# First stage of a float32 layer pair: tile by tile, with x's root applied in the turn, and the values' weights first

## What is computed

```
n = rmsnorm(h, g_mix)          # x * rsqrt(mean(x*x) + EPS) * g
proj = n @ w_in                # 1024 columns in, 6704 out
(b_gate, c_gate, h_conv, q, k_c, v_c, k_s, v_s, k_w, v_w, g_br, g_conv, g_attn) = split(proj)
```

## Time and profile before

| | us |
|---|---|
| median of 3 runs | 745.41 |
| lowest, highest | 744.83, 745.76 |
| the profiled execution's own time | 745.85 |
| its span | 744.1 |
| PE busy in the span | 739.4 (99%) |
| DVE busy, ACT busy | 517.9 (70%), 415.9 (56%) |

### The profile page before, as it was taken

The page is one execution under the profiler, slowest core; times in us unless marked ns, Lnnn a source line. Parts: engine busy times, 40 slices in busy tenths (PEclk is TensorE's granted clock), DMA queues, the critical chain, the costliest instruction groups (busy, mean ns, idle before and its releaser), DMA issues.

```text
span 744.1 us, 11570 instructions
## 1 busy us (share of the span) xinstructions
PE 739.4 (99%) x4557; PEld 640.3 (86%) x4557; DVE 517.9 (70%) x834; ACT 415.9 (56%) x788; POOL 66.5 (9%) x103
## 2 busy tenths in 40 slices
PE   9999999999999999999999999999999999999998
PEld 8999989877788888888888888887888888888886
DVE  5784777795756677887367757898667777447762
ACT  6475557456454456565356547697646656346640
POOL 7300000000010000530000004400100000000000
PEclk9999999999999999999999999999999999999999
DMA  8998454343355546656655562735355655656511
GB/s 261 296 316 270 94 116 147 113 151 114 133 170 197 182 150 219 201 211 227 190 174 203 170 226 60 253 117 179 109 166 170 195 200 175 221 169 193 203 57 56
DMA packets 99209, 131.26 MB, mean 176 GB/s; under 512 B 5357, under 2 KB 79163, under 8 KB 99156
## 3 DMA queue, kind: packets, MB, share of 16 engines
q1 hardware_dynamic: 96564, 125.58, 52.5%
q0 software_dynamic: 2304, 4.43, 2.7%
q10 hardware_dynamic: 288, 0.52, 0.2%
HBM read 128.68 MB, written 1.84 MB: 175 GB/s over the span
## 4 chain that ended last, share of the span: by engine, by line
PE 97%; DVE 2%; ACT 1%; issue 0%; POOL 0%; POOLq 0%
PE B L1631 39%; PE B L1597 22%; PE B L1602 11%; PE B L1586 11%; PE B L1812 2%; PE B L1859 2%; PE B L1822 2%; PE B L1644 1%; PE B L1695 1%; DVE LO L1007 1%; PE B L1638 1%; PE B L1815 1%; PE B L1839 1%; PE B L1740 1%; PE B L1798 0%; PE B L1739 0%
## 5 line engine op out<-in xcount | busy, mean ns | idle before, releaser
L1007 DVE TENSOR_TENSOR LO<-RAW,HI 128x1024 fp32r<-128x1024 f32 x236 | 282.4, 1235 | 100.7 <-ACT HI L543 100.2
L1631 PE MATMUL B<-HI,AA 128*128 128x512 f32 (+1 forms) x960 | 286.4, 376 | 0.3 <-DVE AA L1013 0.2
L543 ACT ACTIVATE HI<-RAW 128x1024 fp32r<-128x1024 f32 (+1 forms) x240 | 236.9, 1038 | 61.4 <-PE B L1631 57.8
L1631 PEld LDWEIGHTS B<-HI,AA 128*128 128x128 f32 x960 | 175.7, 188 | 33.0 <-issue 1.1
L1597 PE MATMUL B<-AA,HI 128*128 128x512 f32 x704 | 179.2, 393 | 0.0
L1631 PE MATMUL B<-LO,AA 128*128 128x512 f32 (+1 forms) x480 | 178.5, 372 | 0.0
L1597 PEld LDWEIGHTS B<-AA,HI 128*128 128x128 f32 x704 | 126.7, 189 | 23.0 <-issue 0.7
L1631 PEld LDWEIGHTS B<-LO,AA 128*128 128x128 f32 x480 | 90.6, 189 | 14.7
L1602 PEld LDWEIGHTS B<-AA,LO 128*128 128x128 f32 x704 | 96.6, 190 | 7.1
L1602 PE MATMUL B<-AA,LO 128*128 128x256 f32 x704 | 98.8, 282 | 0.0
L1586 PE MATMUL B<-AA,HI 128*128 128x256 f32 x448 | 83.1, 286 | 0.0
(11 more groups left out here) (313 smaller groups left out, 634.1 us busy)
## 6 DMA issues: line engine op xcount, KB each, us to landing
RAW<-in_w_in SPq DMA_DIRECT2D x29, 1024.0 KB, 5.5
RAW<-in_w_gate SPq DMA_DIRECT2D x22, 1024.0 KB, 5.4
RAW<-in_w_up SPq DMA_DIRECT2D x22, 1024.0 KB, 5.4
RAW<-in_w_down SPq DMA_DIRECT2D x22, 1024.0 KB, 5.0
RAW<-in_w_in SPq DMA_DIRECT2D x10, 512.0 KB, 6.3
RAW<-in_w_attn_out SPq DMA_DIRECT2D x4, 1024.0 KB, 5.1
RAW<-in_w_o SPq DMA_DIRECT2D x4, 1024.0 KB, 5.0
RAW<-in_w_out SPq DMA_DIRECT2D x4, 1024.0 KB, 5.0
```

Of the source, the lines that this page charges most:

```text
L543: e.activation(pieces(HI, NSPL, i, k), pieces(RAW, NRAW, i, k), ACT.Copy).then_inc(split_hi, 1)
L1007: e.tensor_tensor(pieces(LO, NSPL, i, k), pieces(RAW, NRAW, i, k), pieces(HI, NSPL, i, k), ALU.subtract).then_inc(split_lo, 1)
L1631: x = e.matmul(dst, a, w[:, t, c0:c0 + n], start=(first and t == 0 and k == 0), stop=(last and t == nk - 1 and k == 2))
```

## The change

- x's quarters and unit 0 are transferred in another order and by other queues: SP takes x(0,1), the gain row, x(1,0), x(1,1) and the second half of unit 0; ACT's queue takes x(0,0) and then the first half of unit 0.
- Unit 0 is now the values' weights; the keys' is unit 1, and all up to the values' old place move by one.
- Means and roots are made for each tile apart. The root's factor is no longer multiplied into `TOK`; DVE multiplies it into the identity (`root_turner`: PT is 128x128), and PE's turn is a float32 matmul of TOK with that diagonal (`first_turn`), not a transpose. The turns go by tile: (0,0), (0,1), (1,0), (1,1).
- PE makes the values first, in quarters of 4 products by tile, half of x and kind (AH x hi, AH x lo, AL x hi), twelve quarters of 4; the bias rows stand between two of them. The keys follow as 6 groups of 8. `idle` has 9, 1 and 3 where it had 14, 3, 7 and 3.
- On POOL both roots now stand ahead of the transfers into VR.
- The values at the end of the queries are gone; the first piece of `fill()` is made there instead, ahead of the waits for the queries' copies, and step 0 of the loop makes one piece where it made two.

```diff
@@ SP
-            for h in range(2):
-                e.dma_start(X[:, 0, halves(h)], A["x"][0, 0:128, halves(h)]).then_inc(x_in[h], 16)
-                if h == 0:
-                    e.dma_start(GAIN[0:128:64, :], ...
+            e.dma_start(X[:, 0, halves(1)], A["x"][0, 0:128, halves(1)]).then_inc(x_in[1], 16)
+            e.dma_start(GAIN[0:128:64, :], ...
...
-                    e.dma_start(dst[:, 0:4, :], src[:, 0:4, :]).then_inc(unit0_in, 16)
+                    for h in range(2):
+                        e.dma_start(X[:, 1, halves(h)], A["x"][0, 128:256, halves(h)]).then_inc(x_in[2 + h], 16)
@@ ACT
-            for t, h in ((0, 0), (1, 0), (0, 1)):
-                e.wait_ge(x_in[2 * t + h], 16)
-                squares(2 * t, X[:, t, :], QK[:, t, :], h)
+            e.wait_ge(x_in[0], 16)
+            squares(0, X[:, 0, :], QK[:, 0, :], 0, squares0_sb)
             hi(0, 0)
...
+            turned(0, B[5], 0, 0)
+            e.wait_ge(x_in[2], 16)
+            squares(2, X[:, 1, :], QK[:, 1, :], 0, squares_sb, 3)
+            e.wait_ge(x_in[3], 16)
+            squares(2, X[:, 1, :], QK[:, 1, :], 1)
+            turned(1, B[6], 4, 0)
             hi(0, 1)
@@ DVE
+            mean(0).then_inc(mean_sb, 1)
+            e.wait_ge(gain_pe, 1)
             gained(0, 0)
+            root_turner(0)
+            gained(0, 1)
+            lo(0, 0)
+            turned(0, B[5], 0, 0)
+            gained(1, 0)
             e.wait_ge(squares_sb, 4)
+            mean(1).then_inc(mean_sb, 1)
             gained(1, 1)
+            root_turner(1)
+            turned(1, B[6], 4, 0)
             lo(0, 1)
@@ PE
+            first_turn(0)
+            first_turn(1)
+            idle(3)
+            quarter(0, 0, AH, hi, True)
+            quarter(0, 0, AH, lo)
+            quarter(0, 0, AL, hi)
+            e.matmul(B[4][0:4, 0:ROW], REL[:, :], OH[:, :], start=True, stop=True).then_inc(rel_pe, 1)
+            quarter(0, 1, AH, hi)
+            first_turn(2)
+            first_turn(3)
+            quarter(0, 1, AL, hi)
+            quarter(1, 0, AH, hi, True)
+            quarter(1, 0, AH, lo)
+            quarter(1, 1, AH, hi)
+            quarter(0, 1, AH, lo, last=True).then_inc(vals_pe, 1)
+            quarter(1, 1, AH, lo)
...
-            for t in range(2):
-                values(U_VALS, 0, t)
...
+            filler = fill()
+            next(filler)
             e.wait_ge(q_sb, 8)
...
-                for _ in range(FILL_AT[i]):
+                for _ in range(FILL_AT[i] - (i == 0)):
```

More of the change, by code:

```diff
@@ L530, in _ @@
             own = Own(e, act_step)
-            for h in range(2):
-                e.dma_start(X[:, 1, halves(h)], A["x"][0, 128:256, halves(h)]).then_inc(x_in[2 + h], 16)
+            e.dma_start(X[:, 0, halves(0)], A["x"][0, 0:128, halves(0)]).then_inc(x_in[0], 16)
+            src, nk, n = units[0][0:3]
+            dst = RAW[0][:, 0:nk * n].rearrange("p (t n) -> p t n", t=nk)
+            e.dma_start(dst[:, 0:4, :], src[:, 0:4, :]).then_inc(unit0_in, 16)
             def hi(i, k=None):
@@ L1046, in _ @@
-            e.tensor_scalar(TOK[:, 0, halves(0)], TOK[:, 0, halves(0)], ST[:, 6:7], None, ALU.mult).then_inc(scaled_sb, 2)
-            gained(1, 1)
[L1048 to L1052, removed]
+                e.tensor_tensor(TOK[:, t, halves(h)], X[:, t, halves(h)], B[2 + h][:, :], ALU.mult).then_inc(scaled_sb, 1)
@@ L1652, in _, with first_turn @@
             x.then_inc(gain_pe, 1)
[L1653 to L1665, removed]
+            idle(1)
+            def first_turn(n):
+                t, h = n // 2, n % 2
+                e.wait_ge(scaled_sb, n + 1)
+                e.wait_ge(root_diag, t + 1)
+                take(5 + h, turn_lo, n + 1)
+                for j in range(4):
+                    x = e.matmul(B[5 + h][:, 128 * j:128 * j + 128], TOK[:, t, 512 * h + 128 * j:512 * h + 128 * j + 128],
+                                 PT[:, t, 0:128], start=True, stop=True)
+                x.then_inc(turn_pe, 1)
             def keys(i, br, c):
@@ new lines, in _, with quarter @@
+            hi, lo = view(HI, U_VALS), view(LO, U_VALS)
+            def quarter(t, h, a, w, first=False, last=False):
+                d = slice(t * 128, t * 128 + 128)
+                for c in range(4 * h, 4 * h + 4):
+                    x = e.matmul(B[t][:, 0:256], a[:, c, d], w[:, c, :], start=(first and c == 0), stop=(last and c == 7))
+                return x
+            first_turn(0)
+            first_turn(1)
+            idle(3)
+            take(0, vals_sb, 1)
+            e.wait_ge(split_hi, 1)
@@ new lines, in _ @@
+            first_turn(2)
+            first_turn(3)
+            e.wait_ge(turn_lo, 2)
+            quarter(0, 1, AL, hi)
+            take(1, vals_sb, 2)
+            e.wait_ge(turn_hi, 3)
+            quarter(1, 0, AH, hi, True)
+            quarter(1, 0, AH, lo)
+            e.wait_ge(turn_hi, 4)
+            quarter(1, 1, AH, hi)
+            unit_ready(U_VALS, 1)
+            quarter(0, 1, AH, lo, last=True).then_inc(vals_pe, 1)
+            quarter(1, 1, AH, lo)
+            for h in range(2):
+                e.wait_ge(turn_lo, 3 + h)
+                x = quarter(1, h, AL, hi, last=True)
@@ new lines, in _ @@
+            x.then_inc(vals_pe, 1)
+            hi, lo = view(HI, U_KEYS), view(LO, U_KEYS)
+            e.wait_ge(split_hi, 2 * U_KEYS + 2)
+            for k, (w, a) in enumerate(((hi, AH), (hi, AL), (lo, AH))):
+                if k == 2:
+                    unit_ready(U_KEYS, 1)
+                for c in range(2):
+                    if k == 0:
+                        take(c, keys_sb, c + 1)
+                    for t in range(8):
+                        x = e.matmul(B[c][:, 0:S], w[:, t, 128 * c:128 * c + 128], a[:, t, :], start=(k == 0 and t == 0),
+                                     stop=(k == 2 and t == 7))
+                    if k == 2:
+                        x.then_inc(keys_pe, 1)
```

180 lines of the change are left out of this document (82 added, 98 removed).

## The result

| | before | after |
|---|---|---|
| median of 17 runs, us | 745.67 | 746.61 |
| lowest, highest | 744.83, 746.47 | 745.17, 748.22 |
| profiled execution, its span | 745.85, 744.1 | 747.23, 745.5 |

The ratio is 1.0015, with a 95% interval from 1.0008 to 1.0022. So the changed kernel is slower by about 0.9 us. The forecast was 745.0, a small gain. The difference stays within the 0.2% that the prediction called no change and the median lies within the range, but the sign was wrong. Worth as much notice is the spread: 3.0 us where it was 1.6.

What follows compares the result with a forecast made beforehand. PE was taken to bound the kernel, with 97% of the last-ending chain. Keys done at 25.5 against 25.97 gave a gain of 0.4 to 0.5 us, so 745.0 was forecast; the range with rivals was 743.5 to 747.4.

Steps and rivals of the forecast that it cites:

- G: Time at which DVE may start with the spread gain: forecast 6.9 us, bounds 6.4 and 7.8, against 8.12 before.
- the first needed product: PE's first value products, after two turns and idle(3): forecast to start at G + 3.8 = 10.7 us, against 13.14 before.
- the bank's wait: PE, behind 8 keys products, waits for ACT's second values copy to free bank B1: a new wait of 0.55 us.
- the keys: End of the keys' products at the start: forecast 25.5 us, against 25.97 for keys and values before.
- rival 2: Start transfers: gain row lands late, at 6.7, or the half unit does; 745.4 to 746.1 us; chance 0.17 with another rival.
- The hoisted fill piece: At the queries' end, one fill piece (2.9 us) covers the last copy (0.4); softmax still covered, nothing given back or gained.
- The point from which all is counted: Prediction's heading for deriving G from idle passes, a clock rise near 6.2 us and the gain row's landing at 5.3.
- rival 1: At the start, PE's breaks delay the clock's rise to about 13.5 us: 2.4 us lost, 747.7 us; chance 0.18.
- The 0.2125 of a pass: Duration of early idle passes, 5.95 / 28 us, read as the low clock; 18 passes were to end at 4.9.
- later short waits before 13.14 did not bring the clock down: Argument against rival 1, from PE's start in the kernel before; no size of its own.
- the dearer turns: PE's float32 matmul turns: 1.0 us each against 0.55 as transposes; the two in the needed stream take 0.9 more.
- in terms: Account of the start: stream 2.4 us earlier, less turns 0.9, bias rows 0.73, bank's wait 0.55, less 0.2 of old waits.

Runs made afterwards that it cites:

- e1_busy: Changed kernel with idle(11) for idle(9) ahead of the gain row's wait and idle(4) for idle(1) before the first turn; median 745.77 us, ratio 1.0008.
- e7_before_idle9: Kernel before with idle(9) for idle(14) and idle(1) for idle(3) around the gain products, nothing else; median 746.44 us, ratio 1.0013.
- e8_all: Changed kernel with idle(10) and idle(3), bias rows replacing idle behind turn two, values' copies before unit 2's, earlier bias transfer; median 744.65 us, ratio 0.9994.
- e6_vals_copy: Changed kernel with ACT's copies of both values ahead of its two copies of unit 2; median 746.67 us, ratio 1.0009.

## Why the prediction was wrong, point by point

**Right.** The structure of the sum. In the execution whose clock rose once, every main step is as forecast: the gain row at 5.3, G 6.75 (6.9), the first needed product at 10.47 (10.7), the bias rows 0.74 (0.73), the bank's wait 0.4 (0.55), the keys at 25.18 (25.5), the execution 745.02 (745.0). The transfers were covered as said: the first half unit was copied from 5.91 on (6.12 in the changed kernel's trace), so the half unit's late landing of rival 2 did not come, nor did the row's late landing. The rows' transpose did not wait. The hoisted fill piece gave nothing back.

**The step that failed** is the clock's, under "The point from which all is counted" and in rival 1: I took the one rise of the one trace of before, near 6.2, for a property of the stretch, and gave its course in the changed kernel 0.45 against 0.18 for a loss. In 27 executions the forecast course, by time and mean clock, came 5 times. 15 had the mean clock of a fall, at the low level for about the time of the first two turns, and 7 were slower still, by the traces of the edited kernels a late rise. Measured term: the turns and idle(3) from 7.50 to 11.82 are 4.32 us in place of 2.75, so 1.57 of the error; G being 0.45 earlier than forecast gives some back, and the stretch behind was 0.08 shorter: together 1.04, the difference between 25.5 and 26.54.

A reading beside it was wrong too. The 0.2125 of a pass is a mean over 28 passes of which the last ran at the upper level; it is 1.7 times 0.126, not near 2. At the low level alone 18 passes took 4.21, 0.234 each, and end at 5.27 and not at 4.9. So the first of the two stops that rival 1 names is hardly there unless the clock has risen before it.

**Rival 1** had the right mechanism in the wrong form. I let a break only put off the first rise; what the traces with a fall show is a rise before PE's first stop and then a fall about the end of the last. That the stops bring the fall is shown by e1_busy, where it is gone without them, and by e7_before_idle9, where they bring it to the kernel before. The late rise that I forecast, near 13.5 at 747.7, fits the third group (748.0 to 748.9) and the traced rises near 13; but e8_all had it without a stop, so the reason that I gave for it does not hold. The price was stated as 2.4 us, and measured at 1.64 for the fall, with 746.6 for that group. The sentence that "later short waits before 13.14 did not bring the clock down" was a poor argument: in the kernel before, those waits lay between idle products put there in number. The kernel before with 9 and 1 showed it: it fell in its trace, and by the mean clock in ten of 11 runs. The Trainium skill, "TensorE: Matmul & The Clock Gate", Part 1, says that the point of the rise varies between runs; the traces agree, with 28 idle passes in 5.95 and in 5.21 for the same kernel.

**Not in the prediction at all:** the loop's wait of 0.6 us (0.85 with what follows it) in the profiled execution. It made the two profiles differ by 1.4 us where the medians differ by 0.9. Whether the change has a part in it stays open.

**In the sum, but easy to miss:** the dearer turns. The account "in terms" names 0.9 for the two that stand in the stream; the two ahead of the first product, on the path too, are in the 3.8 from G. With transposes for all four the kernel is 1.3 to 1.5 faster at the median. The bank's wait was put at 0.55, though its own rows (13.7 against 13.25) give 0.45; it measured 0.4.

## What to carry to other kernels

Products that do nothing can be holding the clock. Whoever cuts them, or puts a wait among them, has to price a fall of TensorE's clock: here 1.6 us, more than the 0.4 to 0.5 that the reordering was to win. A late rise cost about 3 us, and came in variants with more idle products too. One trace of a kernel's start shows one course of several; look at the mean granted clock of every run, and at the duration of equal passes, before the course is taken for a property. And a step moved into a stream that is already full costs its whole length, even if it was free where it stood.

## What the runs showed of the hardware that was not expected

- The granted clock column is 1.00 before the first rise, though the passes there take 0.234 us (18 in 4.21) and not 0.126. In the two traced executions with a late rise (747.46 and 747.14) it shows nothing at all; only durations do: gain products 2.10 and 2.01 and not 1.15, turns 3.75 and 3.41 and not 2.02.
- After the clock had reached its upper level it fell again about the end of the second break: at 7.7 in the changed kernel, where PE was at work again from 7.50, and at 7.5 in its second trace, just before PE resumed at 7.55. PE was then busy without a stop, and the clock stayed low until 11.1 and 10.9.
- By the passes' durations the clock stayed low through 11.6 us of unbroken work of PE in e8_all (1.1 to 12.7), while in the other traces without a fall, the late one of e6_vals_copy apart, the passes were at their shorter duration by 7.5.
- A 768 KB transfer from 4 partitions to memory took 34.8 to 35.8 us in all traces, and the 1024 KB units of weights issued while it was under way took 10.2 to 34.3 us from issue to landing, where the 22 such units of each of two later matrices took a median of 5.4.
